# Gate projection of the last mixer's latents, on scaled residual tiles ahead of their normalisation

## The reference

```python
def rms_norm(x, g):
    y = xf * lax.rsqrt(jnp.mean(xf * xf, axis=-1, keepdims=True) + EPS)
    return y * g

def modulate(h, shift, scale):
    return h * (1 + scale) + shift

hx = modulate(rms_norm(x, norm1_g[l]), mod_x[0], mod_x[1])
zx = jnp.split(hx @ w_in[l], N_PARTS, axis=-1)       # ten parts of 256 columns
a_val, a_gate, q, _, _, u, sv, bg, cg, xin = zx
glu = a_val * jax.nn.sigmoid(a_gate)
```

## Time and profile before

| | |
|---|---|
| median of 3 runs | 2423.62 us (2422.07 to 2425.42) |
| span of the profiled execution, first to last instruction | 2420.9 us |
| TensorE busy | 2324.4 us, 96% |
| VectorE busy | 1686.3 us, 70% |
| ScalarE busy | 1011.8 us, 42% |
| mean granted clock of TensorE | 0.990 |
| g0out1, its first to its last matmul | 1974.17 to 2061.38 us |
| first product of kv1 | 2085.47 us |

### The profile page before, as it was taken

How to read it: one execution, slowest core, us unless ns; L and a number is a source line. 1 busy time by engine, 2 the same in 40 slices (tenths; PEclk the granted TensorE clock), 3 DMA queues, 4 the chain that set the end, 5 groups by cost and what they waited for, 6 DMA issues and landing times.

```text
span 2420.9 us, 31471 instructions
## 1 busy us (share of the span) xinstructions
PE 2324.4 (96%) x12378; PEld 1950.3 (81%) x12378; DVE 1686.3 (70%) x2755; ACT 1011.8 (42%) x1585; POOL 31.5 (1%) x65
## 2 busy tenths in 40 slices
PE   7999999999999999999899999899999999989998
PEld 4888878877787888887788999667788888768998
DVE  7776567456588886778768778687675455776665
ACT  3332232256634322224555555655431332465543
POOL 0000000010000000000000000000000000000000
PEclk9999999999999999999999999999999999999999
DMA  8355535542442454443314564212245344323553
GB/s 350 107 203 204 187 139 199 184 174 105 150 164 89 156 182 174 142 140 118 126 53 140 183 199 154 70 53 79 94 164 205 130 181 174 101 70 105 192 183 132
DMA packets 99420, 360.33 MB, mean 149 GB/s; under 512 B 11128, under 2 KB 14584, under 8 KB 97352
## 3 DMA queue, kind: packets, MB, share of 16 engines
q1 hardware_dynamic: 94888, 341.46, 40.5%
q0 software_dynamic: 4384, 16.86, 2.1%
HBM read 350.94 MB, written 5.24 MB: 147 GB/s over the span
## 4 chain that ended last, share of the span: by engine, by line
PE 80%; DVE 11%; ACT 5%; issue 2%; DMA 1%; SPq 1%; DVEq 0%; ACTq 0%
PE PS L607 62%; PE PS L635 3%; PE PS L808 3%; DVE w_lo L1886 3%; PE PS L1024 2%; ACT w_hi L1240 2%; PE PS L850 1%; PE PS L1215 1%; PE PS L824 1%; DVE conv L2692 1%; DMA raw<-in_weights 1%; ACT probs L1748 1%; PE PS L1139 1%; PE PS L954 1%; DVE h_lo L2308 1%
## 5 line engine op out<-in xcount | busy, mean ns | idle before, releaser
L1886 DVE TENSOR_TENSOR w_lo<-raw,w_hi 128x1024 fp32r<-128x1024 f32 (+1 forms) x456 | 543.3, 1210 | 287.6 <-ACT w_hi L1240 286.2
L1240 ACT ACTIVATE w_hi<-raw 128x1024 fp32r<-128x1024 f32 (+1 forms) x456 | 460.7, 1041 | 481.1 <-PE PS L607 443.5
L607 PE MATMUL PS<-h_hi,w_hi 128*128 128x256 f32 (+1 forms) x1472 | 481.6, 335 | 7.5 <-DVE h_lo L2308 3.7
L607 PE MATMUL PS<-h_hi,w_lo 128*128 128x512 f32 (+1 forms) x1416 | 475.6, 336 | 0.0
L607 PE MATMUL PS<-h_lo,w_hi 128*128 128x512 f32 (+1 forms) x1352 | 457.7, 339 | 0.0
L607 PEld LDWEIGHTS PS<-h_hi,w_hi 128*128 128x128 f32 x1472 | 273.6, 188 | 37.9 <-DVE w_lo L1886 4.6
L607 PE MATMUL PS<-hid_hi,w_hi 128*128 128x512 f32 (+1 forms) x864 | 289.7, 335 | 1.9 <-DVE w_lo L1886 1.9
L607 PEld LDWEIGHTS PS<-h_hi,w_lo 128*128 128x128 f32 x1416 | 266.7, 188 | 28.2
L607 PE MATMUL PS<-hid_lo,w_hi 128*128 128x512 f32 (+1 forms) x864 | 288.9, 334 | 0.0
L607 PE MATMUL PS<-hid_hi,w_lo 128*128 128x512 f32 (+1 forms) x864 | 288.7, 334 | 0.0
L607 PEld LDWEIGHTS PS<-h_lo,w_hi 128*128 128x128 f32 x1352 | 254.8, 188 | 28.1 <-issue 0.2
(11 more groups left out here) (434 smaller groups left out, 3754.5 us busy)
## 6 DMA issues: line engine op xcount, KB each, us to landing
raw<-in_weights SPq DMA_DIRECT2D x434, 512.0 KB, 4.5
ada_ring<-in_ada SPq DMA_DIRECT2D x176, 512.0 KB, 3.7
raw<-in_weights SPq DMA_DIRECT2D x22, 384.0 KB, 4.1
qk<-in_ada SPq DMA_DIRECT2D x4, 1024.0 KB, 11.2
xv<-in_ada SPq DMA_DIRECT2D x8, 512.0 KB, 12.6
m_hi<-h_spill POOLq DMA_DIRECT2D x4, 1024.0 KB, 8.1
wgt<-in_x SPq DMA_DIRECT2D x2, 1024.0 KB, 19.8
h_spill<-h_hi POOLq DMA_DIRECT2D x1, 2048.0 KB, 7.5
```

The lines of the kernel that those rows point to most:

```text
L607: mm = pe.matmul(out, a, b, start=(k == 0 and i == 0), stop=(k == ph.k_tiles - 1 and i == 2))
L1240: act.activation(w_hi[:, s, 0:w], raw[:, s, 0:w], ACT.Copy).then_inc(sem("w_hi"), 1)
L1886: dve.tensor_tensor(w_lo[:, s, 0:w], raw[:, s, 0:w], w_hi[:, s, 0:w].bitcast(F32), ALU.subtract)\
```

## The change

**What it does.** VectorE makes the modulation of the last layer's first 16 columns of `mod` before `g0out1`, and puts the shift as two extra columns behind the tiles of `late_hi` and `late_lo` (`late_shift`). During `g0out1` ScalarE makes behind each square `late_hi = X * scale` for the latents, and VectorE `late_lo` (`late_aside`). TensorE runs `zg1` on these tiles: k 0 to 2 between the linear and the product with ones, k 3 to 5 and then 6 and 7 behind it. Each of the four results has 258 columns; ScalarE copies the first extra one as `late_bias`, VectorE multiplies by `r` into `z`, ScalarE adds the bias. These steps stand inside `h_tiles` for this layer. `kv1` now waits for `h_lo` tile by tile. The filler behind the product with ones is gone, and GpSimd's loads of the tables wait for the end of `zg1`, since the new tiles lie in their place.

```diff
@@ (two_stacks, block.gpsimd)
-                pool.wait_ge(sem("tile_done"), LIN["zg1" if l else "kv0"].t0)
+                pool.wait_ge(sem("tile_done"), LIN[f"kv{l}"].t0)
@@ (block.tensor)
+            def late_product(i, k):
+                ph = LIN["zg1"]
+                (g, m), (c, kk), t = divmod(i, 2), divmod(k, 4), ph.t0 + i
+                u, at = ph.u0 + 2 * g + c, slice(kk * ph.width + m * P, kk * ph.width + (m + 1) * P)
+                if m == 0 and kk == 0:
+                    pe.wait_ge(sem("w_split"), u + 1)
+                if k == 0:
+                    freed, n = TILES[t - BANKS]
+                    pe.wait_ge(sem(f"free_{freed}"), n)
+                w, x = (w_hi[:, w_slot(u), at], w_lo[:, w_slot(u), at]), (late_hi[:, k, 0:FOLD_WIDTH], late_lo[:, k, 0:FOLD_WIDTH])
+                for p, (a, b) in enumerate(((w[0], x[0]), (w[0], x[1]), (w[1], x[0]))):
+                    mm = pe.matmul(PS[:, t % BANKS, 0:FOLD_WIDTH], a, b, start=(k == 0 and p == 0), stop=(k == 7 and p == 2))
...
+            def late_products(ks):
+                for k in ks:
+                    pe.wait_ge(sem("late_lo"), k + 1)
+                    for i in range(4):
+                        late_product(i, k)
...
                     linear(name, hi, lo, **more)
+                    if name == "g0out1":
+                        pe.wait_ge(sem("late_columns"), 1)
+                        late_products(range(3))
                     pe.wait_ge(sem("var"), ncall[0])
...
-                if name not in ("g1out1", "f1out1"):
+                if name not in ("g1out1", "f1out1", "g0out1"):
...
-                    front(("zg1",), *hl, ("h_lo", 8 * 6))
-                    linear("zg1", *hl)
-                    linear("kv1", *hx(True))
+                    late_products(range(3, OUTER))
+                    pe.wait_ge(sem("late_lo"), 8)
+                    for i in range(4):
+                        for k in range(OUTER, 8):
+                            late_product(i, k)
+                    linear("kv1", *hx(True), each=("h_lo", 8 * 6))
@@ (block.scalar, squares_behind)
                     split_to(ph.u0 + min(g + 1, 4) * ph.nch + LEAD)
+                    if name == "g0out1" and g == 4:
+                        split_to(LIN["zg1"].u0 + RING - 1)
                     for t in (2 * g - 2, 2 * g - 1) if g else ():
                         act.wait_ge(sem("free_dve"), ph.free0 + t + 1)
                         square(X[:, t, r], T if full else CTX)
+                        if name == "g0out1":
+                            act.activation(late_hi[:, t, 0:CTX], X[:, t, LAT], ACT.Copy, scale=mod[:, 1, 8 + t, 0:1])\
+                                .then_inc(sem("late_hi"), 1)
+
+            def late_bias(i):
+                t = LIN["zg1"].t0 + i
+                act.wait_ge(sem("tile_done"), t + 1)
+                act.activation(small[:, 24 + i:25 + i], PS[:, t % BANKS, CTX:CTX + 1], ACT.Copy).then_inc(sem("late_bias"), 1)
+
+            def late_shifted(i):
+                j = (0, 2, 1, 3)[i]
+                act.wait_ge(sem("late_bias"), i + 1)
+                act.wait_ge(sem("late_scaled"), i + 1)
+                act.activation(z[:, j, LAT], z[:, j, LAT], ACT.Identity, bias=small[:, 24 + i:25 + i]).then_inc(sem("free_act"), 1)
+
+            def late_beside(t):
+                if t in (2, 3):
+                    late_bias(2 * t - 4)
+                    late_bias(2 * t - 3)
+                if t in (3, 4):
+                    late_shifted(2 * t - 6)
+                    late_shifted(2 * t - 5)
...
-                    phase("zg1", copy_to(lambda i: z[:, (0, 2, 1, 3)[i], LAT], False))
+                    only_split("zg1")
@@ (block.vector)
+            def late_low(t):
+                dve.wait_ge(sem("late_hi"), t + 1)
+                dve.scalar_tensor_tensor(out=late_lo[:, t, 0:CTX], in0=X[:, t, LAT], scalar=scalar(1, 1, t, 0),
+                                         in1=late_hi[:, t, 0:CTX].bitcast(F32), op0=ALU.mult, op1=ALU.subtract).then_inc(sem("late_lo"), 1)
...
+            def late_aside(i):
+                if i == 5:
+                    split_to(LIN["zg1"].u0 + RING - 1)
+                if i:
+                    late_low(i - 1)
+
+            def late_beside(t):
+                for i in {1: (0, 1), 2: (2, 3)}.get(t, ()):
+                    bank = (LIN["zg1"].t0 + i) % BANKS
+                    dve.wait_ge(sem("late_bias"), i + 1)
+                    dve.tensor_tensor(z[:, (0, 2, 1, 3)[i], LAT], PS[:, bank, 0:CTX], RSTD[:, LAT], ALU.mult).then_inc(sem("late_scaled"), 1)
...
-                    residual(f"{tag}out{half}", full, par, 5, "squares" if half else None)
+                    if tag == "g0" and half:
+                        gains = (V2["norm1_g_2"] + 8, V2["norm2_g_2"] + 8)
+                        modulation(3, 0, 16, gains=gains)
+                        late_shift()
+                    residual(f"{tag}out{half}", full, par, 5, "squares" if half else None,
+                             late_aside if tag == "g0" and half else None)
...
-                    gains = (V2["norm1_g_2"] + 8, V2["norm2_g_2"] + 8)
-                    modulation(3, 0, 16, gains=gains)
-                    modulation(3, 16, 48, 1, gains)
+                    late_low(7)
+                    modulation(3, 16, 48, 1, (V2["norm1_g_2"] + 8, V2["norm2_g_2"] + 8))
```

More of the change, by code:

```diff
@@ L376, in two_stacks @@
                 hid_lo = sb("hid_lo", [P, 16, T], F32R, inner)
-                turn_lo = sb("turn_lo", [P, 8, CTX], F32R, inner)
+                with ExitStack() as early:
+                    turn_lo = sb("turn_lo", [P, 8, CTX], F32R, early)
+                late_hi = sb("late_hi", [P, 8, CTX + 8], F32R, inner)
+                late_lo = sb("late_lo", [P, 8, CTX + 8], F32R, inner)
             with ExitStack() as inner:
@@ L702, in folded_product @@
                     mm.then_inc(sem("unit_used"), 1)
+            def late_product(i, k):
[10 more added lines that the diff above has]
+                    mm = pe.matmul(PS[:, t % BANKS, 0:FOLD_WIDTH], a, b, start=(k == 0 and p == 0), stop=(k == 7 and p == 2))
+                if k == 7:
+                    mm.then_inc(sem("tile_done"), 1)
+                elif m == 1 and kk == 3:
+                    mm.then_inc(sem("unit_used"), 1)
+            def late_products(ks):
[3 more added lines that the diff above has]
+                        late_product(i, k)
             def residual_product(name, hi, lo, full, mean, beside=None, **more):
@@ L1469, in centred, with h_tiles @@
                 act.activation(RSTD[:, r], RSTD[:, r], ACT.Exp, scale=-0.5).then_inc(sem("rstd"), 1)
-            def h_tiles(n_h, full, chunk, par, following=None):
+            def h_tiles(n_h, full, chunk, par, following=None, beside=None):
                 for t in range(8):
@@ L1475, in h_tiles @@
                         split_to(LIN[following].u0 + RING)
+                    if beside:
+                        beside(t)
                     act.wait_ge(sem("h_made"), 8 * n_h + t + 1)
@@ L1710, in rms @@
                 root(RSTD[:, r], 5, r, D, RMS_SUMS.get(n_h))
-                h_tiles(n_h, full, chunk, par)
+                h_tiles(n_h, full, chunk, par, beside={6: late_beside}.get(n_h))
             item = [16]
@@ L2328, in h_tiles @@
                         split_to(LIN[following].u0 + RING)
+                    if beside and t < 7:
+                        beside(t)
                 lo(7)
@@ L2629, in rms @@
                 rstd(n_h > 4)
-                h_tiles(n_h, full, par, chunk)
+                h_tiles(n_h, full, par, chunk, beside={6: late_beside}.get(n_h))
             def mlp(tag, full, par):
```

9 lines of the change are left out of this document (8 added, 1 removed).

## The result

| | before | after |
|---|---|---|
| median, both kernels on one chip | 2423.55 us (2422.07 to 2425.42) | 2439.46 us (2439.17 to 2441.57) |
| span of the profiled execution | 2420.9 us | 2437.4 us |
| mean granted clock of TensorE | 0.990 | 0.984 |
| g0out1, first product to one step (0.23 us) behind the start of the last | 87.05 us | 99.39 us |
| first product of kv1, counted from E, the last evacuation | 24.06 us | 24.64 us |

The changed kernel is slower: the ratio of after to before is 1.0069, with a 95% interval of 1.0055 to 1.0082, or 13 to 20 us. The forecast was 2437.0, range 2431 to 2441, so the time lies in it, 2.5 above the forecast. What follows goes through the trace in the order of the prediction.

What follows compares the result with a forecast made beforehand. The prediction took TensorE as the bound, 80% of the span. Stops 7.90, their clock 3.20, later kv1 0.50 and its clock 1.90 made 13.5 on 2423.6, said as 2437.0 us, range 2431 to 2441.

Steps and rivals of the forecast that it cites:

- Two stops of 3.95: In g0out1 at units 6 and 10, TensorE waits for split weights behind late_low, 3.95 us each, 7.90 in all.
- The clock in these stops, 3.2: TensorE at half clock around the two g0out1 stops loses 1.6 us each, ends 0 and 2.0.
- From E to the tiles, 0.16 earlier: After g0out1, the ones product ends at E+5.12 against E+5.28, so normalised tiles start at E+6.52, 0.16 us earlier.
- The chain of tiles, 3.35: VectorE's normalised tiles, with gate scales and waits between, take 3.35 us more; last low half ends at E+23.2.
- kv1 starts 0.5 later: First product of kv1 at E+24.56 instead of E+24.06, 0.5 us later.
- (b): Rival: kv1 starts at E+12.1 at the tiles' pace and ends 8.3 us earlier; chance 0.03.
- The clock at kv1, 1.9: After 12 us of idle, half clock at the start of kv1 loses 1.9 us, ends 1.0 and 3.2.
- The sum: Whole kernel: 7.90 + 3.20 + 0.50 + 1.90 = 13.5 us slower.
- (a): Rival: the g0out1 stops are hidden, only the stage behind E counts, 0.5 + 1.9, total 2426.0 us; chance 0.07.
- (d): Rival: a third stop in g0out1, between groups 3 and 4, total 2442.5 us; chance 0.03.
- (c): Rival: TensorE's clock holds through the two g0out1 stops, total 2433.9 us; chance 0.05.

Runs made afterwards that it cites:

- e1: Changed kernel with late_low(0) and (1) moved behind tile 2, late_low(2) and (3) behind tile 4; 2424.44 us, ratio 1.001.
- e3: Kernel before plus only late_hi for tiles 0 to 3 and late_low for tiles 0 to 2 in g0out1, read by nobody; 2438.41 us, ratio 1.0064.
- e6: Changed kernel with filler matmuls, 16 calls ahead of each g0out1 stop and 48 ahead of kv1; 2431.09 us, ratio 1.0032.
- e8: Changed kernel with late_low placed so that only the first stop, at unit 6, is left; one run, g0out1 93.76 us.
- e9: Changed kernel with late_low placed so that only the second stop, at unit 10, is left; one run, g0out1 92.76 us.
- e4: e1 with the first two units of kv1 split among the normalised tiles instead of behind them; 2418.29 us, ratio 0.9979.
- e5: e1 with all four kv1 units split among the tiles and kv1 going k tile by k tile over its four results; 2416.34 us, ratio 0.9967.
- e7: e1 with late_bias, the shifts and VectorE's multiplications from PSUM two tiles later; ratio 1.0008.

## Why the prediction was right, and where it was off

The mechanism and both places were right, and e1 and e3 show it from both sides. Step by step:

- **Two stops of 3.95.** Measured 3.78 of idle, 3.94 counted from product to product, 7.9 for both with 7.90 forecast. The order that was read from the instruction rows, square behind the high half and `late_low` ahead of the low half, was the whole of it.
- **The clock in these stops, 3.2.** This is the term that was mis-sized: it measured 4.1 (e6 against after) to 4.5 (the windows). The forecast put each stop between two rows of before and gave both 1.6. The first cost 2.75, above the upper end of 2.0, the second 1.75, inside. The rows of before had losses of 2.0 and 1.45, and I took them for a scale on which a longer idle costs more. e8 and e9 show two equal idles with costs that differ by 1.0, so the length of the idle doesn't give the price, and the upper end should have been wider: even the sum, 4.1 to 4.5, lies above the 4.0 of the forecast's ends.
- **From E to the tiles, 0.16 earlier.** Measured 0.03 later, E+6.71. The 36 late products start at E-0.2 and take 4.46 us on the chain, where 36 steps of 120 ns gave 4.3. The steps are 0.12 as forecast, but the tenth product and the one behind it came 0.16 late, with the bank of tile 7: the forecast had put that product at E+1 and the bank at E+0.9, free in time, and both met at E+0.9. That is most of the difference. The ones product held at full clock, as forecast. The Trainium skill, "TensorE: Matmul & The Clock Gate", section "Back-to-back issue gap", gives N/2.4 + 2.5 ns as the gap of a matmul by itself at full clock; for 258 columns that is 110 ns, and 3.96 us for the 36 as an estimate. The steps of 0.12 in this trace do not agree, and the measurement decides.
- **The chain of tiles, 3.35.** Measured: last low half at E+23.3 against E+20.0, 3.3.
- **kv1 starts 0.5 later.** Measured 0.6. Rival (b), that kv1 follows its wait, is right as a mechanism only if the weights are there. e4 and e5 make it so, and their three stages are 5.0 and 9.9 us shorter than those of before; the 8.3 worked out for it lie between.
- **The clock at kv1, 1.9.** Measured 1.5 (and 2.8, 2.6 in e1 and e8, 1.4 in e9, 1.6 in e7 after 10.8 of idle); the range given, 1.0 to 3.2, held all of them.
- **The sum.** The stages say 14.5, with 13.5 forecast; the difference is the clock in g0out1 (+1.3) less that at kv1 (-0.4), and a tenth elsewhere. The medians are 15.9 apart. In the profiled execution 1.96 us more had gone before g0out1 began, in code which the change doesn't touch. That the clock term came out too small in g0out1 and too large at kv1, so that the two offset each other in part, is luck. The range has a slip of sum: 2440.2 and the 1.8 for the runs make 2442.0, not 2441.

Rivals (a), hidden stops, and (d), a third stop, did not occur; (c), a clock that holds, held for the whole idle of the second stop and fell behind it, which the idle times alone would not have shown.

## What to carry to other kernels

When work is put on two engines "beside" a busy one, look at what stands behind the new wait on its engine, and not at how long the new work takes: here 0.5 us of VectorE's work, waiting for something that ScalarE made late because it could afford to, held up the low half that TensorE needed, and 12 us were lost; moved behind the next tile the same work was free. A product moved ahead of a wait gains nothing until what the next phase needs (here its split weights) is moved ahead as well: with the stops taken out, the change alone was at or a little above the kernel before, and with kv1's weights ahead it was 8 us below. (Whether they would bring as much without the change was not tried.) And both could be read from the order of the instructions and three timelines, before any run.
